# Inverse softmax sums of a pair of heads: written as 64 equal columns and transposed, instead of diagonals multiplied by ones

## The reference, cut to what matters

```python
p = jax.nn.softmax(jnp.concatenate([l_sel, l_own], axis=-1), axis=-1)
p_sel = p[..., :n_sel * MOBA_BLOCK].reshape(B_, H, Q_BLOCK, n_sel, MOBA_BLOCK)
p_own = p[..., n_sel * MOBA_BLOCK:]
return (jnp.einsum('bhqjk,bhqjkd->bhqd', p_sel, v_sel)
        + jnp.einsum('bhqk,bhkd->bhqd', p_own, v_own))
...
mix = jnp.einsum('bse,ed->bsd', jnp.concatenate([a, r], axis=-1), w_o[l])
```

## Time and profile before

| | us |
|---|---|
| three runs | 632.57, 632.93, 634.10; median 632.93 |
| the profiled execution, whole | 632.15 |
| its span in the profile | 630.3 |
| TensorE products (PE) busy | 606.2 (96%) |
| TensorE weight loads (PEld) busy | 485.6 |
| VectorE (DVE) busy | 478.8 |
| ScalarE (ACT) busy | 374.4 |
| GpSimd (POOL) busy | 133.8 |
| mean granted TensorE clock | 0.987 of full |

### The profile page before, as it was taken

One profiled execution on the slowest core, in us unless ns is written; L12 is line 12 of the kernel. 1 busy time (PEld: TensorE's weight loads), 2 busy tenths in 40 slices (PEclk: granted clock), 3 DMA queues, 4 the chain that ended last, 5 costly groups with the idle time before them and its releaser, 6 DMA issues.

```text
span 630.3 us, 9947 instructions
## 1 busy us (share of the span) xinstructions
PE 606.2 (96%) x3781; PEld 485.6 (77%) x3781; DVE 478.8 (76%) x572; ACT 374.4 (59%) x401; POOL 133.8 (21%) x111
## 2 busy tenths in 40 slices
PE   9999999999999999999799999899999999999991
PEld 7878787887777778887678888688888888888870
DVE  3758498893567575465898988788898888888957
ACT  3659433432125786121568778678777877888735
POOL 0004222390000353000285523111101111111000
PEclk9999999999999999999799999999999999999997
DMA  9831133224206000977599999999999999999554
GB/s 328 280 118 66 41 125 123 68 74 73 68 1 201 3 2 5 399 294 289 182 335 418 419 366 376 390 401 406 398 391 390 389 389 390 404 408 395 180 167 133
DMA packets 42559, 155.79 MB, mean 247 GB/s; under 512 B 11940, under 2 KB 12148, under 8 KB 30237
## 3 DMA queue, kind: packets, MB, share of 16 engines
q1 hardware_dynamic: 37500, 138.40, 56.2%
q0 software_dynamic: 5024, 16.92, 10.4%
HBM read 139.96 MB, written 15.34 MB: 246 GB/s over the span
## 4 chain that ended last, share of the span: by engine, by line
PE 77%; DMA 10%; issue 4%; DVE 4%; POOL 3%; ACT 1%; DVEq 0%; POOLq 0%; ACTq 0%
PE psum L660 21%; PE psum L662 19%; PE psum L661 19%; DMA acc_dram<-misc,slots 6%; PE psum L669 2%; PE psum L773 2%; DMA misc<-x_dram,slots 2%; PE psum L883 2%; PE psum L872 2%; PE psum L909 2%; PE psum L1055 2%; DMA ring<-acc_dram 1%; DMA slot_dram<-rec_i,addr_i 1%; POOL misc L582 1%; PE psum L1072 1%
## 5 line engine op out<-in xcount | busy, mean ns | idle before, releaser
L1777 DVE TENSOR_TENSOR w_lo<-ring,w_hi 128x2048 fp32r<-128x2048 f32 x95 | 216.7, 2298 | 23.3 <-ACT w_hi L1347 23.2
L660 PE MATMUL psum<-w_hi,act_hi 128*128 128x512 f32 x544 | 220.2, 405 | 1.5 <-DVE act_lo L1936 1.0
L662 PE MATMUL psum<-w_hi,act_lo 128*128 128x512 f32 x544 | 212.7, 391 | 0.0
L661 PE MATMUL psum<-w_lo,act_hi 128*128 128x512 f32 x544 | 212.3, 390 | 0.0
L1347 ACT ACTIVATE w_hi<-ring 128x2048 fp32r<-128x2048 f32 x96 | 182.2, 1916 | 25.1 <-PE psum L662 25.1
L660 PEld LDWEIGHTS psum<-w_hi,act_hi 128*128 128x128 f32 x544 | 102.3, 188 | 28.5 <-DVE w_lo L1777 4.5
L662 PEld LDWEIGHTS psum<-w_hi,act_lo 128*128 128x128 f32 x544 | 102.1, 188 | 22.2
L661 PEld LDWEIGHTS psum<-w_lo,act_hi 128*128 128x128 f32 x544 | 102.3, 188 | 18.8
L614 POOL DMA_INDIRECT acc_dram<-misc,slots x15 | 25.8, 1722 | 196.9 <-ACT misc L1397 179.9
L1195 ACT ACTIVATE w_hi<-ring 128x2048 fp32r<-128x2048 f32 x17 | 32.6, 1918 | 49.8 <-PE psum L662 49.3
L1506 DVE TENSOR_TENSOR w_lo<-ring,w_hi 128x2048 fp32r<-128x2048 f32 x17 | 39.8, 2344 | 20.4 <-ACT w_hi L1195 20.1
(11 more groups left out here) (246 smaller groups left out, 705.4 us busy)
## 6 DMA issues: line engine op xcount, KB each, us to landing
ring<-in_w_gate SPq DMA_DIRECT2D x32, 1024.0 KB, 14.6
ring<-in_w_up SPq DMA_DIRECT2D x32, 1024.0 KB, 16.7
ring<-in_w_down SPq DMA_DIRECT2D x32, 1024.0 KB, 14.7
ring<-in_w_in SPq DMA_DIRECT2D x13, 1024.0 KB, 5.2
ring<-in_w_o SPq DMA_DIRECT2D x4, 1024.0 KB, 4.9
acc_dram<-ring SPq DMA_DIRECT2D x5, 512.0 KB
ring<-in_x SPq DMA_DIRECT2D x2, 1024.0 KB, 6.3
ring<-strip_dram SPq DMA_DIRECT2D x8, 256.0 KB, 4.5
```

Of the source, the lines that this page charges most:

```text
L660: pe.matmul(dst, lh, rh, start=first, stop=False, skip_group_check=True)
L661: pe.matmul(dst, lh, rl, start=False, stop=False, skip_group_check=True)
L662: return pe.matmul(dst, ll, rh, start=False, stop=last, skip_group_check=True)
L1777: dve.tensor_tensor(w_lo[:, v0 % WBUF, :], ring[:, slot, :], w_hi[:, v0 % WBUF, :].bitcast(F32), ALU.subtract).then_inc(s_lo, 1)
```

## The change

GpSimd no longer makes diagonals. For each unit it multiplies 64 columns of ones by the column of inverse sums, and the two heads of a pair at one query tile lie side by side in one 128x128 tile of `wide`. TensorE transposes that tile, so the first 64 rows hold the first head's inverse sums and the last 64 the second's: four transposes for a pair in place of eight products. `wide` has two buffers of four tiles, a pair each, in the same place and of the same size as the eight diagonals, so GpSimd waits for TensorE only from unit 16 on, and then for the pair before the last. The semaphore of TensorE's results counts one for each pair instead of two. The places of `spread_scale` in TensorE's list, and those of VectorE's readers, stay.

```diff
-        diag = misc[:, 3072:4096].rearrange("p (n c) -> p n c", c=P)
+        wide = misc[:, 3072:4096].rearrange("p (b i c) -> p b i c", b=2, i=T)
...
-            def inverse_diagonal(n):
+            def inverse_spread(n):
 
                 h, i = unit(n)
                 col = h * T + i
                 pool.wait_ge(s_prec, n // 2 + 1)
-                if n >= DIAGS:
-                    pool.wait_ge(s_scale, 2 * (n // DIAGS))
-                pool.tensor_scalar(diag[:, n % DIAGS, :], ident, prec[:, col:col + 1], None, ALU.mult).then_inc(s_diag, 1)
+                if n >= 4 * T:
+                    pool.wait_ge(s_scale, n // (2 * T) - 1)
+                pool.tensor_scalar(wide[:, n // (2 * T) % 2, i, 64 * (h % 2):64 * (h % 2) + 64], ones[:, 0:64], prec[:, col:col + 1], None, ALU.mult).then_inc(s_wide, 1)
...
             def spread_scale(a):
 
-                pe.wait_ge(s_diag, 2 * T * (a + 1))
+                pe.wait_ge(s_wide, 2 * T * (a + 1))
                 if a >= 1:
                     pe.wait_ge(s_mixa, 2 * a)
                 for i in range(T):
-                    for par in range(2):
-                        last = pe.matmul(psum[64 * par:64 * par + 64, (a + 1) % 2, i * P:(i + 1) * P], ones[:, 0:64], diag[:, 2 * i + par, :],
-                                         start=True, stop=True, skip_group_check=True)
-                        if i == T - 1:
-                            last.then_inc(s_scale, 1)
+                    last = pe.transpose(psum[:, (a + 1) % 2, i * P:(i + 1) * P], wide[:, a % 2, i, :], ident)
+                last.then_inc(s_scale, 1)
...
             def scale_kept(a):
 
-                dve.wait_ge(s_scale, 2 * (a + 1))
+                dve.wait_ge(s_scale, a + 1)
                 dve.tensor_copy(scale_row, bank((a + 1) % 2)).then_inc(s_mixa, 1)
```

More of the change, by code:

```diff
@@ L48 @@
 EARLY = 4
-DIAGS = 8
 UNIT = 2048
@@ L321, in build @@
         s_tab, s_strip, s_stripsb, s_stripd, s_strips = sem("s_tab"), sem("s_strip"), sem("s_stripsb"), sem("s_stripd"), sem("s_strips")
-        s_score, s_logit, s_prob, s_diag, s_pt, s_ptsb, s_pv = sem("s_score"), sem("s_logit"), sem("s_prob"), sem("s_diag"), sem("s_pt"), sem("s_ptsb"), sem("s_pv")
+        s_score, s_logit, s_prob, s_wide, s_pt, s_ptsb, s_pv = sem("s_score"), sem("s_logit"), sem("s_prob"), sem("s_wide"), sem("s_pt"), sem("s_ptsb"), sem("s_pv")
         s_mixt, s_mixthi, s_mixtlo = sem("s_mixt"), sem("s_mixthi"), sem("s_mixtlo")
@@ L569, in inverse_diagonal @@
                 pool.wait_ge(s_prec, n // 2 + 1)
-                if n >= DIAGS:
-                    pool.wait_ge(s_scale, 2 * (n // DIAGS))
-                pool.tensor_scalar(diag[:, n % DIAGS, :], ident, prec[:, col:col + 1], None, ALU.mult).then_inc(s_diag, 1)
+                if n >= 4 * T:
+                    pool.wait_ge(s_scale, n // (2 * T) - 1)
+                pool.tensor_scalar(wide[:, n // (2 * T) % 2, i, 64 * (h % 2):64 * (h % 2) + 64], ones[:, 0:64], prec[:, col:col + 1], None, ALU.mult).then_inc(s_wide, 1)
             for n in range(NU):
-                inverse_diagonal(n)
+                inverse_spread(n)
             def gather(e):
```

## The result

| | before | after |
|---|---|---|
| median of 20 runs, us | 632.81 (629.87 to 635.08) | 635.21 (631.65 to 638.15) |
| ratio | | 1.0048, 95% interval 1.0034 to 1.0062 |
| profiled execution, whole / span | 632.15 / 630.3 | 634.73 / 632.9 |
| mean granted clock | 0.987 | 0.983 |
| low clock, mean over runs | 17.8 us | 22.8 us |

Slower: by 2.4 us between the medians (0.38%), by 0.48% in the ratio with its interval, where I forecast 1.1 us less and a range of 630.5 to 633.2. The last row is twice the span times what the mean clock lacks of 1, for each run, since the lower level is half of full; for before it is the mean of all 64 runs up to then.

What follows compares the result with a forecast made beforehand. TensorE was taken to bound the attention: 3.49 us removed less 2.36 us added gave 1.13 us less, GpSimd and VectorE adding 0 on the path, so a median of 631.8 us, range 630.5 to 633.2.

Steps and rivals of the forecast that it cites:

- TensorE's sum: Attention, four places: 3.49 us of products removed, 2.36 us of transposes added, 1.13 us less (ends 0.4 to 1.8).
- rival 1: Attention: transposes pass to `values` without a new pause; gain 1.8 us, 631.1 us; chance 0.14.
- GpSimd and VectorE: Attention: GpSimd operations about 400 ns, its 6.5 us of waiting for TensorE gone; both engines cost 0 on the path.
- Rival 5: Attention: transposes let the clock fall in four places, 3.3 us lost each, 13 us slower, 645 us; chance 0.02.
- everything behind (...) hangs on TensorE's end of it: Behind the attention: later loads, router and experts follow TensorE's end there, so nothing later takes the saving back.
- carrying through of 1.13 us to the span: Whole kernel: TensorE's 1.13 us saving shows in full, span 629.2 us, median 631.8 us.
- rival 3: Expert stage: the 2.7 us wait for gathered rows vanishes too; gain 3.8 us, 629.1 us; chance 0.07.
- rival 2: Attention or expert stage: TensorE's gain turns into a wait; gain 0 to 0.4 us, 632.5 to 632.9; chance 0.19.
- Rival 4: Router stage: the 6.6 us of low clock lasts longer; if twice as long, 2.2 us slower, 635.1 us; chance 0.06.

Runs made afterwards that it cites:

- warm: Both `early` kernels with 42 more filler products in TensorE's router-stage pauses: medians 629.7 us (from the kernel before) and 628.4 us (from the kernel after).
- early: Kernels before and after, each with expert 5's gather issued two accumulates sooner: medians 631.0 us (before) and 627.6 us (after).
- b_count: Kernel before with 98 filler products of 256 columns made 49 of 512, 98 instructions fewer: 634.5 us, ratio 1.0034.
- b_late: Kernel before with one more small GpSimd copy ahead of expert 4's gather: 632.0 us, ratio 0.9997.
- b_late2: Kernel before with two more small GpSimd copies ahead of expert 4's gather: 632.5 us, ratio 1.0008.
- a_tiny13: Kernel after with 13 tiny products ahead of the transposes in each of four places, 104 instructions more: 630.8 us, ratio 0.9986.
- a_count: Kernel after with router fillers half as wide and twice as many, 104 instructions more: 629.9 us, ratio 0.9975.
- a_wide: Kernel after with fillers half as many and twice as wide, as in b_count: 629.2 us, ratio 0.9957.
- a_early: Kernel after with expert 5's gather issued two accumulates sooner: 627.6 us, ratio 0.9908.

## Why the prediction was wrong

**TensorE's sum was right.** 0.59 us a place was predicted and measured, 1.39 against 1.40 for both groups, no second pause, so rival 1 is out. For pair 3, 1.78 against 1.61: the pause of 0.35 us ahead of it, which I took to stand in both versions, is gone, and the first load starts before the products ahead have ended, so start to start counts some of them. Counted from the load ahead, this place takes 2.01 us where it took 2.44 (246.98 to 248.99, 248.27 to 250.71). The end of it: the group behind the last `values` starts at 248.99, 1.7 us sooner than at 250.71, of which 0.4 us was there at the attention's start (203.87 against 204.29). The pair of `warm` kernels gives 1.2 us for the whole change, the sum said 1.13; the `early` pair gives 3.4.

**A reading that was wrong and cost nothing.** I wrote that the trace doesn't agree with the Trainium skill's sentence on column tiles (TensorE: Matmul & The Clock Gate, Part 3: Packing small matmuls), since the 16 instructions take their full 0.87 us. The 0.87 us already contains it. In the trace of before the 16 start in pairs, 6 to 7 ns apart within a pair (217.927 and 217.934, 218.036 and 218.043) and 0.109 us from pair to pair, which is also the distance of one transpose from the next (221.896, 222.006, 222.115), an instruction on the full width with as many moving columns. Two instructions run in the time of one; one by one, 16 would take 1.74 us. The sum holds, since it used the measured 0.055 us.

**GpSimd and VectorE were right.** It was 445 ns an operation where I took 400, waits gone as described, nothing of it on the path. Rival 5 is out as well: windows of the kernel after, the same stretches as the earlier trace rows.

```profile
221.00:230.00 9.00, 9.00 (x91) 6.58 (x90) 6.53 (x25) 7.33 (x24) 3.79 (x8) 1.00 0.01 3
239.00:246.00 7.00, 7.00 (x63) 5.76 (x62) 3.17 (x9) 6.88 (x15) 2.12 (x4) 1.00 0.01 2
```

**The step that failed** is "everything behind (...) hangs on TensorE's end of it", and with it the carrying through of 1.13 us to the span; slower by over 0.3% had a chance of 0.07. It held to the first expert product. Behind it the path is GpSimd's chain of transfers, of which each link has a time of its own: the landing of the records, which took 0.3 to 1 us longer with a code packet in it, and the issue of a gather, which costs 1.0 or 3.1 us by whether VectorE pauses in that tenth of a us. I had the wait at its end in the earlier trace rows and read it as something that could vanish (rival 3) or take the gain back (rival 2), which at most brought the time back to that of before; neither could make it slower. I never asked when the gather behind it is issued and what stands beside it on VectorE; the margin, 0.22 us from 353.45 to 353.67 on one side, was in the trace of before. A row with a margin of 0.2 us on the path was worth a rival of 2 us and more, on both sides.

**What was taken at nothing.** I counted instructions only as time. 96 instructions less on TensorE also means code that is fetched 9 us later, and the edit of the count by itself, b_count, costs 0.34% (0.11 to 0.58), which is most of the 0.48%, though the interval leaves room for a quarter of it or for all. No step of the prediction had a term for it.

**Rival 4** came nearest in time (635.1) and for the wrong reason. In the router the low clock lasted not longer but came in two pieces, 3.3 us on fillers and 3.5 on experts' products. The third piece stands behind the 4.4 us wait, as such a piece does in all six profiles with a wait of 4.2 us or more; of the two with 2.3 us, before has none and b_late has one (399.2 to 402.6), and the profiles without a wait have none there. Over all runs the kernel after has 5.0 us more of low clock, at half a us each 2.5 us, as much as the whole difference. Cause and result are not told apart by that number, and the warm pair, with 3 and 6 us less of it, didn't gain in that measure. But b_count, with the change's count and none of its work, brings the third piece (clock 0.67 in 400 to 404 us) along. Against this rival I also held that the runs of before lay within 1.5 us; those were three, and the 20 lie within 5.2.

**What stays open.** How a packet of 16 KB, which takes 1 us, delays the records by 0.3 to 1 us: the profile gives the coincidence in 17 kernels, not the DMA engine on which they met. Why the unchanged kernel's median stayed when b_late2 lost the pause in its profile: a single profiled execution may hit what others miss, and medians can only be explained where most executions agree. Why the changed kernels without the loss are 1.6 to 3.2 us under the kernel before of their groups (a_tiny13, a_count 2.3, a_wide), more than the 1.1 us of the sum: before waits 2.3 us for expert 5 and these don't. Ahead of that gather before has an accumulate issued in 3.56 us, and the gather comes at 386.15, in a_count at 379.76; what decides that was not tried apart.

## To carry to other kernels

A saving on the busiest engine is worth what the next chain of transfers lets through: follow the first late wait behind the change back to its issues, and look how many tenths of a us each lies from a neighbour's pause (here the profiles show it, the medians don't show its price). An edit that changes the number of instructions moves the fetches of code behind it; before a small loss is put down to the edit, run the old kernel with the same count. And where a gather's index is ready early, issue it early (a_early, 0.9908): that removed the wait on which all the small shifts acted.

## What was not expected of the hardware

- Code packets (q8, 16 KB, about every 27 us in the expert stage) in a full DMA system: the wait for the records' landing went from 6.2-6.6 us to 6.9-7.6 us, and that for the table's load from 4.6-4.9 to 5.7 us, with a packet in it. The Trainium skill (Runtime: NRT & Kernel Launch, Instruction fetch mechanics) describes refills in blocks of 16 KiB, 256 instructions each, as mostly hidden. Size and spacing agree with these traces. The place of one packet went with 0.34% and more of the time here, so not all of it was hidden.
- One GpSimd gather issue: 1.02 us when it began in a VectorE pause of 0.48 to 0.51 us or at its very end, 3.0 to 3.1 us when it came 0.05 to 0.17 us into a VectorE operation of 2.3 us, always ending 3.18 to 3.19 us after that operation's start (eight profiles).
- Float32 products of 64 columns on the two halves of the array start in pairs, 6 to 7 ns apart, a pair each 0.109 us. Even so 16 instructions cost 0.87 us, and four transposes in their place 0.59 us.
- `ones` of 128x64 times a column cost GpSimd 445 ns, against 603 for 128x128: half the columns, three quarters of the time.
